# Short convolution and pool taken into the input projection, columns in another order, weight units spread anew

## The chip, the cores and the metric

The kernel runs on one core of one Trainium2 chip. The metric is the device time of one execution in microseconds (us). The engines are PE (TensorE, matrix products), DVE (VectorE), ACT (ScalarE), POOL (GpSimd) and SP (SyncE, here a queue of DMA issues). They run side by side and wait for each other by semaphores.

## The reference

One inference step of a hybrid decoder layer, for a prompt of 512 tokens and eight samples of one token, all in fp32. All 520 tokens go through the same weights. What matters here:

```python
u = RMSNorm(h) @ W_in                 # 2048 -> 3848 columns
z, xbc, dt, u5, gate_b, gate_c, hv, upool = split(u)
y_ssd = SSD(causal conv of xbc, dt) * silu(z)
y_s5  = S5(u5), gelu, gated by sigmoid(y @ w_glu + b)
y_sc  = gate_b * causal_dwconv(gate_c * hv, 3 taps)
y_pool = (mean over windows 2, 4, 8, 16 of upool - upool) @ pool_w * pool_scale
m = concat of the four, each 512 wide, each RMS-normed
h = h + m @ W_out
mem_k, mem_v = RMSNorm(mem) @ W_k, RMSNorm(mem) @ W_v      # 256 tokens, prompt
h = h + CrossAttention(h, mem_k, mem_v or the samples' caches)
h = h + relu(RMSNorm(h) @ W_up)^2 @ W_down
```

Outputs are y of both groups and the new states, among them the last rows of `gate_c * hv` and of `upool`.

## The kernel before

**The weight pipeline.** A product in fp32 is made of three: high part by high part, high by low and low by high. The weights come in units of 512 KB. SP loads a unit into one of two buffers `raw` (`load`, lines 589 to 640), ACT copies its high part to `whi` (`hi_units`, `hi_slots`, `hi_first`, lines 785, 799 and 790), POOL subtracts to get `wlo` (lines 728 and 734; one of the first units is done by DVE), and PE multiplies. `whi` and `wlo` have four slots each. A unit's load waits until both parts of the unit that was in its buffer are made; ACT waits until PE is done with the slot. Each engine works through its own fixed program, so a step that waits holds up all behind it.

**The beginning.** SP loads the first chunk of the tokens, two weight units, then the other three chunks. PE turns the gains, then the tokens, k = 0 to 15 (lines 1445 to 1450); DVE copies each turned piece to `xT` and makes the low part `xl`; ACT makes the high part `xh` (line 824) and the squares for the norm (`x_squares`, lines 834 and 838). Two steps behind, PE multiplies kk = k - 2 by the first two tiles of the weights (line 1476), four units held at once. ACT makes the last two of these at k = 4 and 5.

**The projection.** Behind that, tile t is 128 columns by 520 tokens in two units of 48 matmuls (line 1391). The loop over n = 4 to 51 on PE, DVE and POOL is one unit each; tile 4 + n // 2 ends at odd n. DVE evicts it from PSUM (`evict_u`: times `rB`, the norm) to `stg`, ACT stores it to DRAM (`uscr`). PE may not begin a tile until the tile before the last is evicted. Columns come in the order S5, then short convolution's B, C and HV, pool, Z, XBC. Into the loop are put the four parts of S5: PE makes weights at S5_A = 8, 16, 24, 32 (n), sums at S5_B = A + 2, rows at S5_C = A + 4 (lines 1530 and 1534); DVE makes the complex states (`s5_states`, at S5_B) from which the rows are made, with the table `turn` of powers, built by `doubling` at n = 5 and 19 us long. POOL makes the parts' input weights.

**Keys and values.** Then 64 units of `w_v` and `w_k` (`kv_units`, line 1553), each 12 matmuls of 512 columns, are spread by hand between the steps of the mixers: the gate of S5 (line 1766), turning, `ea` (line 1800), pool products (line 1810), norms and chunk states. DVE does the convolution of XBC from loaded columns, gates, four short convolutions (`short_conv`, rows loaded back from `uscr` to `scb`), four groups of pool rows (`pool_rows`, loaded back to `pu`), and evictions. Both pairs of buffers have two turns, so the loads of groups 2 and 3 wait for groups 0 and 1. ACT's program mixes weight copies with these loads, with squares and roots.

The end of the loop and of that stretch is `w_out`, from about 765 us on; everything behind is unchanged.

Of the kernel before, what the change touches and what calls it, by code (L numbers as in the profile page):

```python
# [16 lines left out]
F32 = mybir.dt.float32  # L17
# [51 lines left out]
S5_B = [n + 2 for n in S5_A]  # L69
S5_C = [n + 4 for n in S5_A]  # L70
MEM_AT = [45, 47, 49, 51]

# [60 lines left out]
def build(nc, io, consts_ap, outs):  # L133
# [31 lines left out]
    with ctx:  # L165
# [42 lines left out]
        dte = at("dte", [NH, 3, TOK], R_H + 16640)  # L208

# [28 lines left out]
        rho = at("rho", [P, 4, NCH], BU + 22592)  # L238
# [8 lines left out]
        scb = at("scb", [P, 2, 4, 524], R_A + 45824)  # L247
# [14 lines left out]
        pu = at("pu", [P, 2, PH + TOK + 1], BU + 8320)  # L262
        pt = at("pt", [P, 2, PH + TOK + 1], BU + 12608)
        pt2 = at("pt2", [P, 2, PH + TOK + 1], BU + 16896)
        plw = at("plw", [P, GT, P], BU + 21184)
# [146 lines left out]
        s.sc_done = sem("sc_done")  # L412
# [5 lines left out]
        s.sc_in0 = sem("sc_in0")  # L418
        s.sc_in1 = sem("sc_in1")
        s.pu0 = sem("pu0")  # L420
        s.pu1 = sem("pu1")
# [108 lines left out]
        sc_in = (s.sc_in0, s.sc_in1)  # L530
        pu_in = (s.pu0, s.pu1)
# [42 lines left out]
        def in_row(t):  # L574

            return C_U5 + P * t if t < 20 else P * (t - 20)
# [6 lines left out]
        def _(sp):  # L583
# [40 lines left out]
            load_first(1)  # L624
            load_tokens(1)
# [11 lines left out]
            with sp.Fori(1, 10) as p:  # L637
                load_pair(p, io["w_in"], 256 * p + C_U5)
            with sp.Fori(0, 3) as p:
                load_pair(p + 10, io["w_in"], 256 * p)  # L640
            sp.wait_ge(s.s5_y, 4)
            for i in range(2):
                sp.dma_start(mnat[:, i, :], io["mem"][P * i:P * i + P, :]).then_inc(s.mem_in, 16)
            with sp.Fori(3, 5) as p:
                load_pair(p + 10, io["w_in"], 256 * p)
# [130 lines left out]
        def _(act):  # L776
# [62 lines left out]

            act.wait_ge(s.row_tr, 1)  # L840
# [116 lines left out]
            def s5_toeplitz(f):  # L957

                act.wait_ge(s.fp_st, 16 * (f + 2))
                for i in range(LC):  # L960
# [36 lines left out]
            def store_tile(t):  # L997

                act.wait_ge(s.tile_free, t + 1)
                src = stg[:, t % 2, :] if t >= 6 else (sqt[:], ssq[:])[t % 2]  # L1000
                dma(uscr[in_row(t):in_row(t) + P, :], src, pj[t % 2])
# [28 lines left out]
            for T in range(3, T_KV + 1):  # L1030
# [6 lines left out]
                if T == 5:  # L1037
                    act.wait_ge(s.dt_ask, 1)
                    act.activation(dte[:, 1, :], dte[:, 1, :], ACT.Exp).then_inc(s.dt_act, 1)
# [7 lines left out]

            def load_short(i):
                for j, c0 in enumerate((C_C, C_HV, C_B)):
                    o = 2 if j == 0 else 0  # L1050
                    dma(scb[:, i % 2, j, o:o + TOK], uscr[c0 + P * i:c0 + P * i + P, :], sc_in[i % 2])

            def load_pool(i):
                dma(pu[:, i % 2, PH:PH + TOK], uscr[C_POOL + P * i:C_POOL + P * i + P, :], pu_in[i % 2])
# [6 lines left out]
            load_short(0)  # L1061
            load_short(1)
# [1668 lines left out]
```

## Time and profile before

| | us |
|---|---|
| median of 3 runs | 2927.6 |
| lowest and highest | 2925.55 and 2928.62 |
| the profiled execution | 2924.35 |
| its span in the trace | 2922.2 |
| PE busy | 2827.7 (97%) |
| DVE, ACT, POOL busy | 886.3, 784.5, 1193.2 |

The profile shows one execution. The span runs from its first instruction to its last; 2.15 us lie around it. "Granted clock" is the TensorE clock that the chip allowed, as a share of full speed. In the chain of work that ended last each step is followed back to what released it. A wait names the engine, the line that waited and what released it. PE at 97% is a mean: it hides that nearly all idle time lies before 675 us.

### The profile page before, as it was taken

Reading aid. Unit: us, or ns where it says so; the run is one execution under the profiler, and the core shown is the slowest. Engines: PE = TensorE matmul, PEld = TensorE weight load, DVE = VectorE, ACT = ScalarE, POOL = GpSimd, SP = SyncE. Lnnn points to the kernel's source line nnn. Section 1 sums busy time; section 2 is a strip of 40 time slices with the busy share of each in tenths; the row PEclk is TensorE's granted clock in tenths of the full one; section 3 lists DMA queues with packets and bytes.
Section 4 is the critical chain, followed back from the end, with each engine's and each line's share of the span. In section 5 each row is a group of like instructions: output and inputs, shape, how many; then the busy total and the mean of one; then the engine's idle time right before and its main releaser. Section 6 shows DMA issues by size and latency. Waiting matters only on the chain.

```text
span 2922.2 us, 54159 instructions
## 1 busy us (share of the span) xinstructions
PE 2827.7 (97%) x22196; PEld 2699.3 (92%) x22196; DVE 886.3 (30%) x1313; ACT 784.5 (27%) x992; POOL 1193.2 (41%) x516
## 2 busy tenths in 40 slices
PE   7999998789899999999999999999999999999998
PEld 5989997576799988779999999999999999999998
DVE  4666517956522334522211000110001100011223
ACT  5221125234332211222232212222112321133222
POOL 1545334546344322334344444444444444443441
PEclk9999999899999999999999999999999999999999
DMA  6744444535433565533233333323333333333332
GB/s 173 138 114 121 115 137 165 169 130 164 160 100 93 150 202 191 193 103 92 81 101 91 90 91 94 93 87 94 93 91 89 93 93 92 88 93 93 87 92 94
DMA packets 510351, 338.36 MB, mean 116 GB/s; under 512 B 31525, under 2 KB 459411, under 8 KB 508815
## 3 DMA queue, kind: packets, MB, share of 16 engines
q1 hardware_dynamic: 470488, 294.02, 34.3%
q10 hardware_dynamic: 39771, 43.04, 5.0%
q8 instruction: 67, 1.10, 0.2%
q14 instruction: 25, 0.20, 0.0%
HBM read 313.28 MB, written 24.02 MB: 115 GB/s over the span
## 4 chain that ended last, share of the span: by engine, by line
PE 81%; issue 9%; POOL 5%; DVE 3%; DMA 1%; ACT 1%; ACTq 0%; POOLq 0%; SPq 0%; DVEq 0%
PE lin L1391 75%; POOL wlo L728 5%; DMA raw<-in_w_in 1%; PE aux L1644 1%; PE aux L1689 1%; PE lin L1584 1%; PE aux L1635 1%; DVE turn L1965 0%; DVE rot L1965 0%; ACTq L802 0%; PE aux L1534 0%; PE aux L1530 0%; PE lin L1476 0%; DVE ca L1965 0%; PE aux L1956 0%
## 5 line engine op out<-in xcount | busy, mean ns | idle before, releaser
L728 POOL TENSOR_TENSOR wlo<-raw,whi 128x1024 fp32r<-128x1024 f32 x472 | 1139.2, 2416 | 1649.8 <-ACT whi L799 1348.7
L799 ACT ACTIVATE whi<-raw 128x1024 fp32r<-128x1024 f32 x384 | 405.9, 1059 | 1438.4 <-PE lin L1391 1298.4
L1391 PE MATMUL lin<-fl,whi 128*128 128x260 f32 x2048 | 578.4, 282 | 0.0
L1391 PE MATMUL lin<-fh,wlo 128*128 128x260 f32 x2048 | 578.0, 282 | 0.0
L1391 PE MATMUL lin<-ml,whi 128*128 128x260 f32 x2048 | 577.6, 282 | 0.0
L1391 PE MATMUL lin<-fh,whi 128*128 128x260 f32 x2048 | 577.6, 282 | 0.0
L1391 PE MATMUL lin<-mh,whi 128*128 128x260 f32 x2048 | 577.5, 282 | 0.0
L1391 PE MATMUL lin<-mh,wlo 128*128 128x260 f32 x2048 | 577.3, 282 | 0.0
L1391 PEld LDWEIGHTS lin<-fh,wlo 128*128 128x128 f32 x2048 | 385.9, 188 | 0.0
L1391 PEld LDWEIGHTS lin<-mh,wlo 128*128 128x128 f32 x2048 | 385.6, 188 | 0.0
L1391 PEld LDWEIGHTS lin<-ml,whi 128*128 128x128 f32 x2048 | 385.5, 188 | 0.0
L1391 PEld LDWEIGHTS lin<-fh,whi 128*128 128x128 f32 x2048 | 385.3, 188 | 0.0
L1391 PEld LDWEIGHTS lin<-mh,whi 128*128 128x128 f32 x2048 | 385.2, 188 | 0.0
L1391 PEld LDWEIGHTS lin<-fl,whi 128*128 128x128 f32 x2048 | 385.2, 188 | 0.0
L1391 PE MATMUL lin<-xh,whi 128*128 128x260 f32 x896 | 256.3, 286 | 5.9 <-DVE stg L1965 5.9
L1391 PE MATMUL lin<-xl,whi 128*128 128x260 f32 x896 | 254.3, 284 | 0.0
L1391 PE MATMUL lin<-xh,wlo 128*128 128x260 f32 x896 | 254.0, 283 | 0.0
L1965 DVE TENSOR_TENSOR h<-lin,h 128x520 f32 (+1 forms) x96 | 67.2, 700 | 582.3 <-PE lin L1391 573.2
L1965 DVE TENSOR_TENSOR fl<-hsq,fh 128x520 f32 x64 | 72.6, 1135 | 476.7 <-ACT fh L1333 476.7
L1391 PEld LDWEIGHTS lin<-xh,whi 128*128 128x128 f32 x896 | 169.9, 190 | 8.3 <-DVE stg L1965 6.4
L1391 PEld LDWEIGHTS lin<-xh,wlo 128*128 128x128 f32 x896 | 170.0, 190 | 0.0
L1391 PEld LDWEIGHTS lin<-xl,whi 128*128 128x128 f32 x896 | 169.9, 190 | 0.0
(417 smaller groups left out, 4380.1 us busy)
## 6 DMA issues: line engine op xcount, KB each, us to landing
raw<-in_w_up SPq DMA_DIRECT2D x128, 512.0 KB, 4.0
raw<-in_w_down SPq DMA_DIRECT2D x128, 512.0 KB, 3.9
raw<-in_w_in SPq DMA_DIRECT2D x60, 512.0 KB, 3.8
raw<-in_w_v SPq DMA_DIRECT2D x32, 512.0 KB, 3.7
raw<-in_w_k SPq DMA_DIRECT2D x32, 512.0 KB, 3.7
raw<-in_w_out SPq DMA_DIRECT2D x32, 512.0 KB, 3.9
raw<-in_w_q SPq DMA_DIRECT2D x32, 512.0 KB, 4.0
piece<-in_cache_mem_k SPq DMA_DIRECT2D x32, 512.0 KB, 6.1
```

What stands on the lines that cost most here:

```text
L728: pool.tensor_tensor(wlo[:, slot, :], raw[:, slot % 2, :], whi[:, slot, :].bitcast(F32), ALU.subtract).then_inc(s.w_lo, 1)
L799: act.activation(whi[:, slot, :], raw[:, slot % 2, :], ACT.Copy).then_inc(s.w_hi, 1)
L1391: mm = pe.matmul(lin[:, 2 * i + f, 0:HALF], w, m[:, k, HALF * f:HALF * f + HALF], start=(n == 0 and part == 0), stop=(n == KT - 1 and part ...
L1584: mm = pe.matmul(lin[:, 2 * i + f, 0:HALF], w, m[:, k, HALF * f:HALF * f + HALF], start=(k == 0 and part == 0), stop=(k == KT - 1 and part ...
L1635: mm = pe.matmul(aux[32 * j:32 * j + 32, 2, :], pTd[:, m, 32 * b:32 * b + 32], piece[:, j, m, :], start=(g == 0 and m == 0), stop=(g == 1 ...
L1644: mm = pe.matmul(aux[:, 2, 0:NMEM], q[:, f0 + d, P * tt:P * tt + P], kTh[:, d, :], start=(d == 0), stop=(d == 3))
L1689: mm = pe.matmul(aux[:, d % 2, :], vNh[:, m, P * d:P * d + P], pT[:, m, :], start=(m == 0), stop=(m == 1))
L1965: step(v.tensor_tensor(out, a, b, op), sm)
```

## The change

- Order of columns: S5, Z, then C, HV and B of each of the four short-convolution groups in turn, pool, XBC. Only Z and XBC tiles are stored to DRAM: 10 in place of 26.
- The short convolution of group i is done by DVE in the projection, after tiles 9, 12, 15, 18 (n = 11, 17, 23, 29), from tiles evicted straight to `scc` and `scp`; B is multiplied in as its tile is evicted. Pool rows follow tiles 20 to 23 (n = 33, 35, 37, 39); PE does the pool products at n = 37, 39, 41, 43 and DVE evicts them one n later. Loads from DRAM for both are gone.
- S5_B and S5_C of the first part come one unit later, the doubling of `turn` is split over n = 4, 6, 7 and 8, and the state transposes come between the first projection units.
- In the stretch of keys and values the pool products are gone, the units are spread anew (three to a chunk in place of two), sigmoids come in pairs, and squares and roots of the norms stand earlier in ACT's program.
- The beginning: SP waits for the first token chunk before it loads the others; the first weight copy precedes the gains copy, parameters and squares come one step later, the third and fourth copy at k = 8 and 9; DVE makes `xl` of k right after `xT` of k; the first products of kk = 0 and 1 leave out the `wlo` part, which is made up at kk = 2 and 3.

```diff
-S5_B = [n + 2 for n in S5_A]
-S5_C = [n + 4 for n in S5_A]
+S5_B = [11] + [n + 2 for n in S5_A[1:]]
+S5_C = [n + 2 for n in S5_B]
+POOL_AT = [37, 39, 41, 43]
...
+        def in_col(t):
+
+            if t < 4:
+                return C_U5 + P * t
+            if t < 8:
+                return C_Z + P * (t - 4)
+            if t < 20:
+                return (C_C, C_HV, C_B)[(t - 8) % 3] + P * ((t - 8) // 3)
+            return C_POOL + P * (t - 20) if t < 24 else C_XBC + P * (t - 24)
+
+        def stored(t):
+            return 4 <= t < 8 or t >= 24
...
             load_first(1)
+            sp.wait_ge(s.x_in0, 80)
             load_tokens(1)
...
-            hi_first(0)
-            hi_first(1)
             for k in range(KT):
                 x_hi(k)
                 if k == 0:
+                    hi_first(1)
+                if k == 1:
                     parameters()
-                if 1 <= k <= 8:
-                    x_squares(2 * k - 2)
-                    x_squares(2 * k - 1)
-                if k in (4, 5):
-                    hi_first(k - 2)
+                if 2 <= k <= 9:
+                    x_squares(2 * k - 4)
+                    x_squares(2 * k - 3)
+                if k in (8, 9):
+                    hi_first(k - 6)
...
-                if k == 11:
+                if k == 13:
                     root(0)
-                if k == 13:
+                if k == 14:
                     hi_slots(1, (0,))
...
-                    if n % 2 == 1 or n == 6:
+                    if (n % 2 == 1 or n == 6) and stored(2 + (n - 1) // 2):
                         store_tile(2 + (n - 1) // 2)
...
-            for i in range(2):
-                act.wait_ge(pj[i], 16 * 13)
+                act.wait_ge(pj[i], 16 * 5)
...
-                if 1 <= i <= 4:
-                    act.wait_ge(s.glu_mm, i)
...
+                for g in ((i - 1, i) if i in (1, 3) else ()):
+                    act.wait_ge(s.glu_mm, g + 1)
...
-            act.wait_ge(s.sc_done, 1)
-            load_short(2)
-            hi_units(14, 16)
-            act.wait_ge(s.sc_done, 2)
-            load_short(3)
-            hi_units(16, 17)
-            hi_units(17, 18)
+            hi_units(14, 18)
...
+            norm_squares(0, s.glu_y, 1)
+            hi_units(21, 22)
             for f in range(2):
...
-            hi_units(21, 23)
+            hi_units(22, 24)
+            root(1)
+            norm_squares(1, s.tile_free, 20)
+            hi_units(24, 27)
             kv_store(1)
             load_rows(0, 5)
-            for i in (2, 3):
-                act.wait_ge(s.mx_pool, i - 1)
-                pool_tail(i - 2)
-                act.wait_ge(s.tails, i)
-                load_pool(i)
-                hi_units(19 + 2 * i, 21 + 2 * i)
-            hi_units(27, 28)
+            root(2)
+            norm_squares(2, s.pl_ev, 4)
+            hi_units(27, 30)
             load_rows(5, 11)
-            hi_units(28, 30)
+            root(3)
+            hi_units(30, 32)
             load_rows(11, 16)
...
                 if kk == 0:
                     pe.wait_ge(s.par_ev, 7)
+                    pe.wait_ge(s.w_hi, 2)
+                if kk == 2:
                     pe.wait_ge(s.w_lo, 2)
                 if kk == 8:
                     pe.wait_ge(s.w_lo, 4)
...
+                        if kk < 2:
+                            first_products(kk, i, (0, 1))
+                        else:
+                            if 2 <= kk < 4:
+                                first_products(kk - 2, i, (2,))
+                            mm = first_products(kk, i, (0, 1, 2))
...
+            def pool_products(i):
+
+                if i == 0:
+                    pe.wait_ge(s.pl_in, 16)
+                pe.wait_ge(s.mx_pool, i + 1)
+                if i >= 1:
+                    pe.wait_ge(s.pl_ev, i)
+                for f in range(2):
+                    mm = pe.matmul(aux[:, f, 0:HALF], plw[:, i, :], halves(pt[:, i % 2, 0:TOK])[:, f, :],
+                                   start=True, stop=True)
+                mm.then_inc(s.pl_mm, 1)
...
-                kv_units(20 + 2 * i, 22 + 2 * i)
-            kv_units(28, 30)
+            kv_units(20, 22)
             pe.wait_ge(s.ea_act, 4)
             token_sums(1, KT + 4)
-            kv_units(30, 31)
+            kv_units(22, 24)
             token_spread(1)
...
-                kv_units(36 + 2 * c, 37 + 2 * c)
+                kv_units(30 + 3 * c, 31 + 3 * c)
...
-                kv_units(37 + 2 * c, 38 + 2 * c)
+                kv_units(31 + 3 * c, 33 + 3 * c)
...
-            kv_units(44, 46)
+            kv_units(42, 46)
...
-            for k in range(KT + 1):
-                if k < KT:
-                    v.wait_ge(s.x_tr, k + 1)
-                    cp(halves(xT[:, k, :]), x_bank(k), s.x_ev)
-                if k >= 1:
-                    v.wait_ge(s.split_hi, k)
...
+            for k in range(KT):
+                v.wait_ge(s.x_tr, k + 1)
+                cp(halves(xT[:, k, :]), x_bank(k), s.x_ev)
+                v.wait_ge(s.split_hi, k + 1)
...
+                elif t < 20:
+                    i, j = (t - 8) // 3, (t - 8) % 3
...
+                    out = (scc[:], scp[:, 2:2 + TOK], y[:, 8 + i, :])[j]
                 else:
...
+                    out = pu[:, PH:PH + TOK]
+                factor = y[:, 8 + i, :] if 8 <= t < 20 and j == 2 else rB[:]
+                tt(halves(out), lin_tile(t % 2), halves(factor), ALU.mult, s.tile_free)
...
             s5_weights(0)
             for n in range(4, 52):
+                if n == 4:
+                    v.wait_ge(s.xs_st, 64)
+                    doubling(turn, 3, range(3))
+                if n in (6, 7, 8):
+                    doubling(turn, 3, (n - 3,))
+                if n == 9:
+                    state_steps()
                 if n in S5_B:
                     s5_states(S5_B.index(n))
                 if n - 1 in S5_C[0:3]:
                     s5_weights(S5_C.index(n - 1) + 1)
                 if n - 3 in S5_C:
                     s5_y(S5_C.index(n - 3))
                 if n - 1 in MEM_AT:
                     mem_rows(MEM_AT.index(n - 1))
+                if n - 1 in POOL_AT:
+                    pool_out(POOL_AT.index(n - 1))
                 if n % 2 == 1:
+                    tile = 4 + n // 2
+                    evict_u(tile)
+                    if 8 <= tile < 20 and (tile - 8) % 3 == 1:
+                        short_conv((tile - 8) // 3)
+                    if 20 <= tile < 24:
+                        pool_rows(tile - 20, POOL_W[tile - 20])
                 if n == 11:
                     soft_ask()
                 if n in (20, 24, 28, 32):
                     softplus(n // 4 - 5)
```

## Rows read from the trace of the kernel before

**Rows 1.** The page, chain that ended last: shares of the span by engine.

```profile
PE 81%; issue 9%; POOL 5%; DVE 3%; DMA 1%; ACT 1%; ACTq 0%; POOLq 0%; SPq 0%; DVEq 0%
```

**Rows 2.** Stretches: busy time (count) of PE, PEld, DVE, ACT, POOL; clock; DMA share; GB/s.

```profile
0.00:73.00 73.00, 52.49 (x366) 40.68 (x366) 30.98 (x43) 36.88 (x82) 13.12 (x11) 1.00 0.61 174
73.00:186.00 113.00, 104.86 (x890) 102.77 (x886) 81.09 (x157) 27.18 (x37) 56.76 (x29) 0.95 0.61 128
186.00:450.00 264.00, 262.82 (x2312) 258.21 (x2312) 110.72 (x149) 61.03 (x81) 109.42 (x51) 1.00 0.42 118
450.00:520.00 70.00, 60.67 (x276) 49.06 (x276) 59.06 (x84) 38.24 (x45) 33.19 (x14) 0.95 0.60 195
520.00:589.00 69.00, 51.55 (x169) 37.21 (x169) 62.97 (x81) 18.74 (x23) 38.47 (x16) 0.81 0.56 167
589.00:675.00 86.00, 79.33 (x341) 61.17 (x339) 55.28 (x75) 27.78 (x36) 42.62 (x19) 0.94 0.41 135
```

**Rows 3.** Waits of PE, 73 to 186: us in total, times, longest.

```profile
PE lin L1391 <- DVE stg L1965: 5.9, 1, 5.9
```

**Rows 4.** Timeline of DVE near 158: start, duration, line, operation, shapes.

```profile
158.33 0.70 DVE L1965 TENSOR_TENSOR stg<-lin,rB 128x520 f32<-128x520 f32 x1
```

**Rows 5.** Timeline of DVE, 235 to 241, as in Rows 4.

```profile
236.19 2.67 DVE L1965 TENSOR_TENSOR hc<-rot,turn 128x256 f32<-128x256 f32 x1
238.89 0.42 DVE L1965 TENSOR_TENSOR rot<-rot,turn 128x256 f32<-128x256 f32 x1
...
240.02 0.40 DVE L1977 COPY hc<-h 128x32 f32<-128x32 f32 x2
```

**Rows 6.** Timeline of POOL in the same stretch.

```profile
236.18 2.39 POOL L728 TENSOR_TENSOR wlo<-raw,whi 128x1024 fp32r<-128x1024 f32 x1 [4.82 <-ACT whi L799]
```

**Rows 7.** Timeline of PE where these states are taken up.

```profile
240.51 0.63 PE L1530 MATMUL aux<-uc,tw 128*128 128x73 f32 x4
```

**Rows 8.** Timeline of DVE at the third S5 part; brackets: idle before it, releaser.

```profile
281.84 0.70 DVE L1965 TENSOR_TENSOR stg<-lin,rB 128x520 f32<-128x520 f32 x1 [1.73 <-PE lin L1391]
```

**Rows 9.** Timeline of DVE, short convolution 1, from its first product to the next.

```profile
510.23 2.65 DVE L1965 TENSOR_TENSOR scb<-scb 128x520 f32<-128x520 f32 x1
...
516.87 0.70 DVE L1965 TENSOR_TENSOR scb<-scb 128x520 f32<-128x520 f32 x1
```

**Rows 10.** Timeline of DVE, first pool group, to the next one's start.

```profile
553.79 0.07 DVE L2364 MEMSET pu<- 128x15 f32 x1
...
555.78 2.29 DVE L1965 TENSOR_TENSOR pt<-plS,pu 128x8 f32<-128x8 f32 x1
...
558.34 0.07 DVE L2364 MEMSET pu<- 128x15 f32 x1
```

**Rows 11.** Waits of PE, 450 to 675.

```profile
PE lin L1553 <- POOL wlo L728: 10.2, 6, 4.3
...
PE aux L1800 <- DVE smk L1965: 3.9, 1, 3.9
```

**Rows 12.** Groups by line, 450 to 675: count, busy us, mean ns, idle before.

```profile
L728 POOL TENSOR_TENSOR wlo<-raw,whi 128x1024 fp32r<-128x1024 f32 x47 | 116.8, 2492 | 110.7 <-ACT whi L785 107.3 <-ACT whi L799 3.2
...
L785 ACT ACTIVATE whi<-raw 128x1024 fp32r<-128x1024 f32 x44 | 46.0, 1055 | 97.8 <-DMA raw<-in_w_v 33.4 <-DMA raw<-in_w_k 31.7 <-PE lin L1553 15.1
...
L1810 PE MATMUL aux<-pt,plw 128*128 128x260 f32 x16 | 6.6, 552 | 11.5 <-DVE pt L1974 5.8 <-DVE y L1969 5.7
```

**Rows 13.** The page, DMA issues: count, KB, median us from issue to landing.

```profile
raw<-in_w_v SPq DMA_DIRECT2D x32, 512.0 KB, 3.7
```

**Rows 14.** Timeline of PE at the third pool product.

```profile
566.83 1.04 PE L1810 MATMUL aux<-pt,plw 128*128 128x260 f32 x4
```

**Rows 15.** Timeline of PE in the beginning: the first products follow these transposes.

```profile
21.51 0.48 PE L1445 MATMUL aux<-idn,xnat 128*128 128x128 f32 x1 [4.91 <-DVE xl L1974]
```

**Rows 16.** Timeline of ACT in the beginning.

```profile
45.15 0.61 ACT L834 ACTIVATE xsq<-xnat 128x512 f32<-128x512 f32 x1
...
47.86 0.73 ACT L824 ACTIVATE xh<-xT,gains 128x520 fp32r<-128x520 f32 x1
```

More of the change, by code:

```diff
@@ L1126, in _, with norm_squares @@
             act.wait_ge(s.ss_st, 16 * 5)
+            def norm_squares(j, ready, count):
+                act.wait_ge(ready, count)
+                for i in range(4):
+                    act.wait_ge(s.ss_done, KT + 4 * j + max(i - 1, 0))
+                    act.activation((sqt, hsq)[i % 2][:], y[:, 4 * NORM_ORDER[j] + i, :], ACT.Square).then_inc(s.sq_done, 1)
+            norm_squares(0, s.glu_y, 1)
+            hi_units(21, 22)
             for f in range(2):
@@ L1459, in _, with first_products @@
                     mm.then_inc(s.stat_mm, 1)
+                def first_products(kk, i, parts):
+                    slot = 2 * i + kk // 8
+                    wh = whi[:, slot, P * (kk % 8):P * (kk % 8) + P]
+                    wl = wlo[:, slot, P * (kk % 8):P * (kk % 8) + P]
+                    for part in parts:
+                        w, m = ((wh, xh), (wh, xl), (wl, xh))[part]
+                        for f in range(2):
+                            mm = pe.matmul(lin[:, 2 * i + f, 0:HALF], w, m[:, kk, HALF * f:HALF * f + HALF],
+                                           start=(kk == 0 and part == 0), stop=(kk == KT - 1 and part == 2))
+                    return mm
                 kk = k - 2
@@ L1470, in _ @@
                     for i in range(2):
-                        slot = 2 * i + kk // 8
-                        wh = whi[:, slot, P * (kk % 8):P * (kk % 8) + P]
-                        wl = wlo[:, slot, P * (kk % 8):P * (kk % 8) + P]
-                        for part, (w, m) in enumerate(((wh, xh), (wh, xl), (wl, xh))):
-                            for f in range(2):
-                                mm = pe.matmul(lin[:, 2 * i + f, 0:HALF], w, m[:, kk, HALF * f:HALF * f + HALF],
-                                               start=(kk == 0 and part == 0), stop=(kk == KT - 1 and part == 2))
+                        if kk < 2:
[4 more added lines that the diff above has]
+                            mm = first_products(kk, i, (0, 1, 2))
                         if kk == 7 and i == 0:
@@ L1710, in _ @@
             mm.then_inc(s.dt_mm, 1)
-            for n in range(1, 4):
-                w_in_unit(n)
+            w_in_unit(1)
             pe.wait_ge(s.st_in, 80)
@@ L1745, in mem_turn @@
                     mm.then_inc(s.mem_tr, 1)
+            def pool_products(i):
[4 more added lines that the diff above has]
+                    pe.wait_ge(s.pl_ev, i)
+                for f in range(2):
+                    mm = pe.matmul(aux[:, f, 0:HALF], plw[:, i, :], halves(pt[:, i % 2, 0:TOK])[:, f, :],
+                                   start=True, stop=True)
+                mm.then_inc(s.pl_mm, 1)
             for n in range(4, 52):
-                for at_, what in ((S5_A, s5_weights), (S5_B, s5_sums), (S5_C, s5_rows), (MEM_AT, mem_turn)):
+                for at_, what in ((S5_A, s5_weights), (S5_B, s5_sums), (S5_C, s5_rows), (POOL_AT, pool_products),
+                                  (MEM_AT, mem_turn)):
                     if n in at_:
@@ L1892, in _ @@
             pe.wait_ge(s.mixn, 16)
[L1893 removed]
+            pe.wait_ge(s.tails, 1)
             for i in range(4):
@@ L2101, in doubling @@
             def doubling(tabl, k0, steps):
-                step(v.memset(tabl[:, 0, :, 0:1], 1.0))
-                step(v.memset(tabl[:, 1, :, 0:1], 0.0))
-                for k in range(steps):
+                if 0 in steps:
+                    step(v.memset(tabl[:, 0, :, 0:1], 1.0))
+                    step(v.memset(tabl[:, 1, :, 0:1], 0.0))
+                for k in steps:
                     n = 1 << k
```

241 lines of the change are left out of this document (95 added, 146 removed).

## Prediction

> **What bounds the kernel now.** I read the chain of work that ended last first: PE carries 81% of it, POOL and DVE 8% together [rows 1]. So time moves only where PE waits, where it runs at the lower clock, or where it gets more work. The table by stretch says where that is [rows 2]. From 186 to 450 us (projection) PE is busy 262.8 of 264 us at clock 1.00: nothing can be won there, and any wait put in counts fully. From 73 to 186 it is idle 8.1 us at clock 0.95; from 450 to 675 (memory keys and values beside the mixers) 9.3, 17.5 and 6.7 us, together 33.5 us, at 0.95, 0.81 and 0.94. These clocks are means of the two levels 1.2 and 2.4 GHz. The change touches 0 to 675 us alone. Third, the waits of PE by releaser in both stretches [rows 3, 11], and the timelines around each moved step [rows 4 to 10, 14 to 16].
>
> **A price for the clock.** A mean of 0.95 over 113 us is 5.7 us of full-speed work lost, for 8.1 us of idle time, 0.7 per idle us; from 450 to 675 the loss is 3.5 + 13.1 + 5.2 = 21.8 us for 33.5, 0.65 per idle us [rows 2]. Part of that low clock lies in the idle time itself, so 0.65 is an upper end and 0 the lower. I take 0.4 for single waits in dense work and 0.65 in the stretch where waits follow each other.
>
> **Beginning (0 to 73 us): 0, from -5 to +8.** Before, the transposes of k=2 wait 4.91 us for DVE's first low parts, and the first products follow right after [rows 15]. With the first token chunk loaded alone, the gains copy behind only one weight copy, and no `wlo` in the first products, they start 4 to 5 us sooner: -5 is the lower end. But `hi_first(3)` now stands on ACT after k=9 and its squares. ACT before spends 2.7 us on one k's two squares and rows (45.15 to 47.86) [rows 16]; then the copy of 1.06 and POOL's subtraction of 2.5 us [rows 12] come before the wait of kk=8 for the fourth `w_lo`, and the third copy, 1.06, one k earlier. That chain is 7.3 us; PE's own work on one k, which before keeps pace with ACT's 2.7, covers as much of it. A wait of about 4.6 us plus hand-overs takes back what the start gave. DVE also waits for ACT between its two steps of each k now; unknown, and covered by +8.
>
> **First S5 part (73 to 186 us): -10.5.** The 5.9 us wait is for the eviction `stg` at 158.33, queued behind the whole doubling of `turn` [rows 3, 4]. With the doubling spread over n = 4, 6, 7, 8 and S5_B at 11, I take 7.5 of the 8.1 idle us as gone, and 0.4 x 7.5 = 3.0 of clock. Ends: 5.9 and 12.5. The state transposes move between two units and wait for nothing that is late.
>
> **DVE steps moved into the full projection: +30.8, from +14 to +42.** The tiles' stores to DRAM and the loads back vanish, off PE's path, worth 0. What counts is DVE's queue.
> Part 1 of S5: DVE ends the states at 240.42 (240.02 + 0.40) and PE takes them at 240.51 [rows 5, 7]: no slack. `short_conv(1)` (n=17) now stands ahead of them. From its first product to the next one's is 6.64 us, of which 1.95 (2.65 against 0.70) is a stretched operation [rows 9]; so +4.7 clean, 6.6 held. I take 6.5, since POOL subtracts all along here.
> Part 2: DVE idles only 1.73 us before the eviction ahead of these states [rows 8], and `short_conv(2)` comes before: 4.7 - 1.7 = 3.0 to 6.6 and, with a further held operation of 2.1 [rows 10], 8.7. I take 6.
> Part 3: `pool_rows(0)` in front: 4.55 us from start to start, 2.3 less 0.18 of it held [rows 10]: 2.4 to 5.3; I take 5.
> `pool_products(1)` and `(2)` wait for `pool_out`, which is queued behind the next `pool_rows` on DVE; two units are some 11 us (2312 matmuls in 264 us, 48 to a unit [rows 2]), against two `pool_rows` with evictions in that time, so 0 to 6; I take 4.5.
> Sum 22.0, and 0.4 x 22 = 8.8 of clock: 30.8. Only S5's rows and the pool products wait on PE for it; evictions are behind them in the same queue. Low end 10.1 (all clean) x 1.4 = 14, high end 26.6 plus 0.6 of clock each, 42.
>
> Why an operation is held: `hc` with two SBUF inputs took 2.67 us beside a POOL subtraction of 2.39 us that began 0.01 us earlier, its twin right after 0.42 [rows 5, 6]. The Trainium skill (SBUF — State Buffer, the section "SBUF: two separate sides") says that DVE operations with two SBUF inputs and GpSimd operations exclude each other for a whole instruction. The trace agrees, 2.67 against 0.42 us. It speaks against this change: by that rule each POOL subtraction met costs about its own 2.4 us, and the first of the waits above would be 4.7 + 2.4 = 7.1 in place of 6.5, the sum 0.8 more.
>
> **Pool products moved into a stretch that PE fills: +4.2**, four at 1.04 us [rows 14]. They go from the later stretch below.
>
> **Memory keys and values (450 to 675 us): -20.4, from -28 to -7.**
> Gone: the products themselves, 6.6 busy, and their waits, 11.5 [rows 12]; the 3.9 us wait for `smk`, since four short convolutions no longer stand before it on DVE, and of the 10.2 us of waits for `wlo` some 6.4 (4.3 is the longest), since weight copies no longer queue behind pool loads and tails on ACT [rows 11]. Together 21.8 us of waits.
> New: on ACT the weight copies 22, 27 and 30 stand behind eight DMA issues, behind `root(2)` with four squares, and behind `root(3)`. No row shows these; the longest wait that a late `wlo` makes now is 4.3 [rows 11], so 0 to 12.9. I take 11.6, near the upper end, as these units come with fewer other PE steps between them.
> The clock: 0.65 x (21.8 - 11.6) = 6.6 back. Weights must arrive faster than now: +3, from 0 to 6. Sum: -6.6 - 21.8 + 11.6 - 6.6 + 3 = -20.4. Up to about 515 us DVE's convolution paces the stretch, and I give it nothing.
> The floor is the chain of one weight buffer: 3.7 landing [rows 13], 1.06 copy, 2.49 subtraction [rows 12], 7.25 us over two buffers, 3.6 a unit. The stretch takes 225 us for 47 units, 4.8 each, and would take 4.35.
>
> **The sum.** 0 - 10.5 + 30.8 + 4.2 - 20.4 = +4.1 us. The profiled execution took 2924.35 us (span 2922.2, 2.15 around it), 3.25 below the median of 2927.6. So 2924.35 + 4.1 + 3.25 = 2931.7 us.
>
> **The rivals.**
> B: POOL doesn't hold the moved steps, and they cost their bare time. For it: the steps are cheap, and POOL works only 109 of 264 us there [rows 2]. Against: both the convolution and the pool rows measured had a held operation [rows 9, 10]. It gives 14.1 in place of 30.8, and if ACT's order costs 8.6 in place of 11.6, 2931.7 - 16.7 - 3 = 2912.
> C, on the slower side: the stretch of keys and values does not give the time back. With DVE's waits gone, the weight chain and ACT's order set the pace: waits on `pt`, `y` and `smk` turn into waits on `wlo`. It decides once PE asks for a unit faster than about 4.5 us. Gone are then 6.6 + 11.5 + 3.9, new are 11.6 + 3, and no clock comes back: -7.4 in place of -20.4, which is 2944.7. For it: `wlo` is the largest single releaser there already [rows 11]; against: ACT is busy 85 of 225 us, POOL 114 [rows 2].
> D: the beginning doesn't do what the change says: the wait for the fourth `w_lo` costs 8 us more than the start gives, 2939.7. For it: nothing but squares fills ACT there [rows 16].
>
> **How the numbers follow.** A measurement of this kernel can tell 0.2%, 5.9 us, from no change: the band is 2921.7 to 2933.5. My forecast has 0.50, with a range of its own of 2920 to 2944 (its terms' bounds, not all at once): 0.05 faster, 0.24 same, 0.21 slower. B has 0.27 (0.24 faster, 0.03 same), C 0.15 (all slower), D 0.08 (0.01, 0.02, 0.05). That makes 0.30 faster, 0.29 same, 0.41 slower. The range goes from 2902, B with the first S5 part at its end of 12.5 and the beginning at -5, to 2950, C with a beginning that loses 5.
>
> **What would show it.** The beginning: the first product before 20 us, and a wait of about 5 us on `wlo` near 45 us. First S5 part: no wait on `stg` from 73 to 186, the stretch 10 us shorter. Projection: PE waits on `hc` or `s5o` at n = 20, 28, 36 of 5 to 6 us each, and on `y` before the second and third pool product; without these waits B holds. Keys and values: no waits on `pt` and `smk`; if those on `wlo` grow beyond 20 us, C holds. The prediction is wrong if PE waits in the projection stay under 12 us, or if the later stretch shortens by less than 10 or over 30 us.

## The result and the profile after

The change makes the kernel slower: 2958.4 us median of 4 runs (2955.5 to 2961.2) against 2928.1 (2925.6 to 2929.2), a ratio of 1.011 with a 95% interval of 1.0097 to 1.0122. The profiled execution took 2961.2 us, its span is 2959.1; the one before had 2922.2. So the two traces differ by 36.9 us, the medians by 30.3.

The chain that ended last, by engine, in the profile after (before: [rows 1]):

```profile
PE 80%; issue 8%; DVE 5%; POOL 5%; DMA 1%; ACT 1%; SPq 0%; POOLq 0%; DVEq 0%; ACTq 0%
```

DVE's share of the chain has risen from 3% to 5%. The stretches after, columns as in [rows 2]:

```profile
0.00:73.00 73.00, 52.22 (x313) 43.04 (x316) 27.28 (x42) 35.99 (x81) 10.15 (x9) 0.95 0.61 173
73.00:186.00 113.00, 113.00 (x994) 109.76 (x986) 86.39 (x149) 30.62 (x40) 62.36 (x31) 0.97 0.61 130
186.00:450.00 264.00, 233.42 (x1854) 225.62 (x1854) 153.52 (x214) 39.71 (x50) 93.83 (x43) 0.88 0.33 87
450.00:520.00 70.00, 67.07 (x487) 63.74 (x486) 19.91 (x36) 25.46 (x37) 26.25 (x11) 0.95 0.38 122
520.00:589.00 69.00, 63.94 (x287) 49.32 (x286) 52.17 (x71) 35.69 (x45) 35.69 (x16) 0.98 0.42 129
589.00:675.00 86.00, 68.99 (x308) 54.21 (x306) 34.85 (x55) 27.02 (x34) 43.76 (x19) 0.94 0.49 152
```

From 186 to 450 us PE is now busy 233.4 of 264 us, 262.8 before, at a clock of 0.88 in place of 1.00 [rows 2]. That is where the time went. PE waits there for `hc`, the complex states, and for `y`, into which DVE evicts the pool products; before, its waits on `hc` were 0.9 us or less, and there was none on `y`. Now, from 186 to 460 us:

```profile
PE aux L1518 <- DVE hc L1967: 23.6, 4, 6.9
PE aux L1744 <- DVE y L1959: 7.0, 2, 4.9
```

Four waits on `hc`, one for each part of S5, and two on `y`, before the second and third pool product. They are 30.6 us together. From 460 to 765 us:

```profile
PE lin L1541 <- POOL wlo L735: 26.6, 17, 3.8
```

The waits on `pt`, on `y` and on `smk` of [rows 11, 12] are gone, and waits on `wlo` have grown to 26.6 us; before they were 13.4 in the same window. From the first unit of keys and values to the last the stretch went from 308.3 to 293.6 us, but PE still waits 39.1 us in it, 41.2 before: waits on `wlo` took the place of those on DVE. What it gave back is the pool products, 6.6 us, and some 6 us of clock, 0.95 in place of 0.91.

**Where the 36.9 us lie.** The two kernels do the same steps in nearly the same order, so a step's start in both traces tells how far one is behind. I took three: the products for `dt` after the beginning (101.99 before, 105.01 after), the sums of S5's part 0 (172.56 and 172.99; after, one unit more of 5.9 us lies before them), and the first transposes of the memory tokens, which stand at unit 45 in both. The latter in the timeline of PE, before and after:

```profile
405.83 0.93 PE L1744 MATMUL aux<-idn,mnat 128*128 128x128 f32 x7
```

```profile
457.06 0.71 PE L1733 MATMUL aux<-idn,mnat 128*128 128x128 f32 x5
```

| stretch | after less before | predicted |
|---|---|---|
| beginning, to the `dt` products | +3.0 | 0 (-5 to +8) |
| to the sums of part 0 | -8.5 | -10.5 |
| from there to unit 45: moved steps and pool products | +56.7 | +35.0 |
| behind unit 45: keys and values | -14.3 | -20.4 |
| sum | +36.9 | +4.1 |

Three terms are about what was forecast, and one is 22 us off. What stands in it: waits of 30.6 us, less 1.2 that were there before; four pool products, 3.1 (what they add below in the kernel with the same work one unit later, where PE doesn't wait around them); and the rest, 24.2 us, for which PE ran, but at the lower clock.

**How a moved step becomes a wait.** The timeline of DVE around part 1, from the first product of `short_conv(1)` to its last, the start of the states, a held operation among them, and the last copy:

```profile
232.61 0.70 DVE L1955 TENSOR_TENSOR scp<-scp,scc 128x520 f32<-128x520 f32 x1
...
238.52 0.70 DVE L1955 TENSOR_TENSOR y<-y,rB 128x520 f32<-128x520 f32 x1
239.26 0.29 DVE L1967 COPY rho<-s5p 128x256 f32<-128x256 f32 x1
...
246.09 2.54 DVE L1955 TENSOR_TENSOR hc<-rot,turn 128x256 f32<-128x256 f32 x1
...
251.18 0.40 DVE L1967 COPY hc<-h 128x32 f32<-128x32 f32 x2
```

The convolution takes 6.6 us (232.61 to 239.26), the states start behind it and end at 251.58. PE needed them at 244.8. The timeline of PE there, brackets as in [rows 8]:

```profile
251.63 1.13 PE L1518 MATMUL aux<-uc,tw 128*128 128x73 f32 x4 [6.84 <-DVE hc L1967]
252.69 1.13 PE L1522 MATMUL aux<-hc,ca 64*128 64x73 f32 x8
```

It waits 6.84 us, and then each group of the rows takes 1.13 us. Before, the first took 0.63 [rows 7]. The clock in the 8.6 us of these rows and in the 11.8 behind them, columns as in [rows 2]:

```profile
251.60:260.20 8.60, 8.57 (x49) 7.52 (x49) 4.51 (x3) 0.00 (x0) 0.00 (x0) 0.50 0.00 0
260.20:272.00 11.80, 11.80 (x84) 11.80 (x85) 4.55 (x6) 1.78 (x3) 2.39 (x1) 0.83 0.22 47
```

0.50 is the lower of the two levels, 1.2 GHz, and 0.83 a mix of both. The rows take 8.6 us in place of the 4.8 they took before (+3.8), and 0.17 of the next 11.8 us is 2.0 more: 5.8 us for the clock, behind a wait of 6.8.

In part 2 the convolution is not directly ahead of the states, but the queue is: three rows of DVE, the convolution's first product, its last, and the eviction of the next tile:

```profile
285.96 0.70 DVE L1955 TENSOR_TENSOR scp<-scp,scc 128x520 f32<-128x520 f32 x1
...
296.89 0.70 DVE L1955 TENSOR_TENSOR y<-y,rB 128x520 f32<-128x520 f32 x1
...
306.03 0.70 DVE L1955 TENSOR_TENSOR y<-lin,y 128x520 f32<-128x520 f32 x1
```

11.7 us for the convolution (4.7 clean), then 8.4 for the softplus's second part; the states start only at 306.8, 7.2 us after PE's sums were done at 299.6.

Part 0's wait of 5.1 us has no short convolution and no pool rows ahead of it. Ahead are the last two doublings, beside POOL's input weights, and the state steps; three rows of them:

```profile
163.28 1.17 DVE L1955 TENSOR_TENSOR etmp<-turn,ang 128x256 f32<-128x256 f32 x1
...
170.29 2.77 DVE L1955 TENSOR_TENSOR turn<-turn,etmp 128x512 f32<-128x512 f32 x1
...
174.67 2.47 DVE L1955 TENSOR_TENSOR etmp<-h,s5p 128x128 f32<-128x128 f32 x1
```

Operations of 128 x 256 that took 0.43 us before take 1.17 while POOL works through six operations of 1.1 to 1.4 us each; the two others shown are held for 2 us.

### The profile page after: what moved, and what is told of

Its sections match the earlier page's. It is cut to its first block, busy times and chain, and to the rows that moved or that the text cites. A ratio compares the mean times of both kernels' runs of the same rounds, so it can differ in the third digit from the quotient of the medians.

```text
span 2959.1 us, 53927 instructions
## 1 busy us (share of the span) xinstructions
PE 2843.5 (96%) x22196; PEld 2716.6 (92%) x22196; DVE 884.6 (30%) x1311; ACT 776.2 (26%) x984; POOL 1192.5 (40%) x516
## 4 chain that ended last, share of the span: by engine, by line
PE 80%; issue 8%; DVE 5%; POOL 5%; DMA 1%; ACT 1%; SPq 0%; POOLq 0%; DVEq 0%; ACTq 0%
PE lin L1366 73%; POOL wlo L735 5%; PE aux L1632 1%; PE aux L1677 1%; DVE turn L1955 1%; PE lin L1445 1%; PE lin L1572 1%; DVE rot L1955 1%; PE aux L1518 1%; PE aux L1522 1%; PE aux L1623 1%; DVE pt L1955 0%; DVE hc L1955 0%; DMA raw<-in_w_in 0%; DVE etmp L1955 0%
```

## The experiments

All times are medians. Each comparison gives the ratio to the kernel before, run on the same chip. That kernel took 2926.3 to 2928.7 us in the three sets of runs below and 2928.1 above, so a difference in us between kernels of different sets is good to some 2 us, as here between the changed kernel and the others. Two theories were to be told apart first. Theory 1: the steps moved into the projection stand ahead of S5's states in DVE's queue, PE waits, and the clock falls after each wait. Theory 2: the rest of the change, order of columns, positions and products, makes the loss.

**The moved arithmetic left out.** This kernel does not compute the short convolutions and the pool rows, nor the product with B at the eviction; of each step one short operation and the copy of the new state remain.

```diff
             def short_conv(i):
...
-                tt(p[:, 2:2 + TOK], p[:, 2:2 + TOK], scc[:], ALU.mult)
+                cp(o[:, 0:8], p[:, 2:10])
                 cp(scn[:, i, :], p[:, SEQ:SEQ + 10])
-                ts(o[:, 0:SEQ], p[:, 2:2 + SEQ], scw[:, i, 2:3])
...
             def pool_rows(i, w):
...
-                stt(o[:, 0:SEQ], src[:, PH:n], 1.0 / w, u[:, PH:n], ALU.mult, ALU.subtract)
...
+                ts(o[:, 0:TOK], u[:, PH:PH + TOK], 1.0 / w, sm=s.mx_pool)
```

> The changed kernel with the arithmetic of the short convolutions and of the pool rows left out on DVE (one short copy, or one scaling of the tile, stays of each, so all waits and hand-overs are kept; the outputs that hang on them are not computed). Theory 1, DVE's queue: the waits of PE on hc of parts 1 to 3 (6.8, 6.9, 4.8 us) and on y (7.0) go, the one of part 0 (5.1) stays, since no moved step stands ahead of it; with 0.7 us of clock for each that is 25.5 x 1.7 = 43 us, near 2915. Theory 2, the other parts of the change (order of columns, part 0 one unit later, stores and products in other places) make the loss: at most 10 us faster than the changed kernel, 2948 or more.

Measured: 2920.2 us, ratio 0.998 (0.997 to 0.999), 38 us faster than the changed kernel. The waits on `hc` were 4.8 us in part 0 and 1.2, none worth naming and 1.2 in the others, those on `y` were gone. Theory 1 holds: with the other parts of the change all in place, the loss is gone. Theory 2 falls.

**The same work, one unit later.** Nothing is left out here.

```diff
                 if n in S5_B:
                     s5_states(S5_B.index(n))
+                if n in (12, 18, 24, 30):
+                    short_conv(n // 6 - 2)
...
                 if n - 1 in POOL_AT:
                     pool_out(POOL_AT.index(n - 1))
+                if n in (34, 36, 38, 40):
+                    pool_rows(n // 2 - 17, POOL_W[n // 2 - 17])
                 if n % 2 == 1:
                     tile = 4 + n // 2
                     evict_u(tile)
-                    if 8 <= tile < 20 and (tile - 8) % 3 == 1:
-                        short_conv((tile - 8) // 3)
-                    if 20 <= tile < 24:
-                        pool_rows(tile - 20, POOL_W[tile - 20])
```

> The changed kernel with each short convolution and each group of pool rows one unit later in DVE's program, so that they stand behind the complex states of parts 1 and 3; nothing is left out. Theory 1, the place in the queue: the waits on hc of parts 1 and 3 go (6.8 and 4.8 us), part 0 and part 2 keep theirs; 11.6 x 1.7 = 20 us faster, near 2938. Theory 2, the amount of DVE work and POOL's holding set the wait wherever the steps stand: under 8 us faster, 2950 or more.

Measured: 2926.5 us, ratio 1.0008 (0.9998 to 1.0017): 32 us faster than the changed kernel, with the same work. The waits of PE from 186 to 460 us:

```profile
PE aux L1518 <- DVE hc L1967: 12.6, 2, 6.9
```

Parts 0 and 2 are left, 5.8 and 6.9. It gained more than the 20 expected, because both waits on `y` went too (7.0): `pool_out` now stands ahead of the next `pool_rows`. The sum is 18.6 us of waits, and some 13 us of clock, which is the rest and agrees with the traces (13.6 us in the stretches behind these waits). The loss is one of order in a queue.

**The softplus behind the states of part 2.**

```diff
-                if n in (20, 24, 28, 32):
-                    softplus(n // 4 - 5)
+                if n in (20, 27, 29, 43):
+                    softplus((20, 27, 29, 43).index(n))
```

> As the kernel before it in this set, and the second part of the softplus moves from unit 24 to 27, the third to 29 and the fourth to 43, behind the states of part 2 (and 3). Theory 1: the wait on hc of part 2 (6.9 us) goes too, another 11 us, near 2927. Theory 2, part 2 waits for the short convolution ahead of it and not for the softplus: no more than 3 us beyond the kernel before it.

Measured: 2920.1 us, ratio 0.9976 (0.9967 to 0.9986), 6.4 faster than the kernel before it in this set, and faster than the kernel before the change. The waits:

```profile
PE aux L1518 <- DVE hc L1967: 4.6, 1, 4.6
PE aux L1733 <- DVE y L1959: 2.4, 1, 2.4
```

The gain lies between the two theories' 11 and 3 us, but the wait of part 2 is gone, as theory 1 said, and its rows end 10.9 us sooner. A new wait of 2.4 us, before the memory transposes, gave some of it back, the stretch of keys and values the rest.

**What a wait costs, in the kernel before.** Seven scratch operations of 0.76 us ahead of the states of parts 1 to 3:

```diff
+                for _ in range(7 if f else 0):
+                    tt(ctmp[:], ctmp[:], ctmp[:], ALU.max)
                 cp(rho[:], s5p[:, 6, w].unsqueeze(2).to_broadcast([P, 4, NCH]))
```

> The kernel before, and seven more operations of 0.76 us on a scratch tile ahead of the complex states in parts 1, 2 and 3: 5.3 us of DVE work each, more where POOL holds one. It measures what a wait of PE in the full projection costs. PE's waits should be about 5.2, 3.6 and 5 us, 14 in all. Theory 1, a wait costs about 0.7 us of clock for each us: +24. Theory 2, the price of the prediction, 0.4: +19. Theory 3, the wait alone: +14.

Measured: 2970.1 us, ratio 1.015 (1.0133 to 1.0167), +43.7 us (38.3 of it in the stretch of the table below); far above each theory. The waits were 6.8, 8.3 and 6.9 us, not 14 together but 22.0. The same loop with 1, 2 and 4 operations:

> The kernel before with 1, 2 and 4 operations of 0.76 us ahead of the complex states in parts 1, 2 and 3: waits of PE of about 0.7, 1.6 and 3 us. It tells what the clock costs at each length. A price by the us (0.7): 5.3 x 1.7 = +9. A price by the event: nothing after the 0.7 us wait, about 5 us after each of the others, whatever its length, +14 to +16.

Measured: 2953.0 us, ratio 1.0081 (1.0064 to 1.0098), +24.5. The waits were 1.2, 4.6 and 5.5 us. The rows that follow the first two in the timeline of PE:

```profile
243.09 0.67 PE L1530 MATMUL aux<-uc,tw 128*128 128x73 f32 x4 [1.17 <-DVE hc L1977]
243.69 0.67 PE L1534 MATMUL aux<-hc,ca 64*128 64x73 f32 x8
```

```profile
301.82 1.13 PE L1530 MATMUL aux<-uc,tw 128*128 128x73 f32 x4 [4.60 <-DVE hc L1977]
302.88 1.13 PE L1534 MATMUL aux<-hc,ca 64*128 64x73 f32 x8
```

The clock while these rows ran, in the same columns as in [rows 2]:

```profile
243.10:247.90 4.80, 4.80 (x49) 4.20 (x49) 4.73 (x3) 0.00 (x0) 2.35 (x1) 1.00 0.38 116
301.80:310.40 8.60, 8.58 (x49) 7.53 (x49) 4.02 (x7) 0.00 (x0) 0.00 (x0) 0.50 0.31 94
```

After 1.17 us of waiting the rows run at full speed, after 4.60 at half. With 2, 1 and 2 operations:

> The kernel before with 2, 1 and 2 operations of 0.76 us ahead of the states in parts 1, 2 and 3, for waits of about 2, 1.5 and 2.5 us. A price of the clock by the event that sets in above some 1.2 us: each costs 4 to 6 us more than itself, +18 to +24 in all. A price that grows with the wait: +9 to +11.

Measured: 2955.5 us, ratio 1.0092 (1.0072 to 1.0113), +26.8; the waits were 4.1, 3.9 and 4.1 us. The stretch from the end of part 0's rows to the memory transposes took 214.4 us before and in these three kernels:

| kernel | longer by | waits more by | rest, the clock | waits of 3.9 us and more | each |
|---|---|---|---|---|---|
| seven operations | 38.3 | 21.7 | 16.6 | 3 | 5.5 |
| 1, 2 and 4 | 22.2 | 10.9 | 11.3 | 2 | 5.6 |
| 2, 1 and 2 | 27.7 | 11.7 | 16.0 | 3 | 5.3 |

So ahead of S5's rows the clock's price goes by the wait, and not by its length. Taken one by one, from the rows' first matmul to PE's next need of DVE, less what this took before, the eight waits of 3.9 to 8.3 us cost 4.2 to 6.1 us each on top of themselves; the longest cost 5.7, the shortest 6.1. In the changed kernel the four waits on `hc` cost about as much, but the fifth long one, 4.9 us on `y`, only 2.4. Behind it come a pool product and projection matmuls, and no S5 rows. The same holds for the 5.9 us wait on `stg` in the kernel before, which projection matmuls follow. The clock behind each, the kernel before first, then the changed one:

```profile
159.10:163.20 4.10, 4.10 (x19) 4.10 (x20) 3.96 (x5) 3.14 (x5) 2.58 (x2) 0.50 0.35 132
163.20:186.00 22.80, 22.45 (x207) 22.01 (x206) 16.19 (x22) 3.44 (x4) 16.59 (x10) 1.00 0.54 138
```

```profile
429.90:434.90 5.00, 4.96 (x19) 4.60 (x20) 0.00 (x0) 0.00 (x0) 0.00 (x0) 0.50 0.37 104
434.90:445.00 10.10, 10.10 (x85) 10.07 (x85) 1.46 (x2) 1.08 (x2) 2.39 (x1) 1.00 0.17 49
```

PE works 4 to 5 us at half speed there, and loses 2.0 and 2.4 us. Behind the eight waits ahead of S5's rows it works 10.2 to 14.0 us at half speed. The place differs between the two kinds and no run changes it alone, so it isn't shown that the rows are the reason; the traces show only that the two kinds differ.

For short waits the length doesn't decide at all: waits of 1.2 and 1.4 us were followed by no fall in the kernel with 1, 2 and 4 operations and in the last one below. In the one with the arithmetic left out the rows behind two waits of 1.2 us took 7.6 and 6.0 in place of 4.8 us, and from these rows on to PE's next need of DVE it took 4.4 and 3.1 us more.

Why do operations of 0.76 us make a wait of 3.9? The timeline of DVE in part 2 of the last kernel:

```profile
292.05 1.42 DVE L1965 TENSOR_TENSOR ctmp<-ctmp 128x576 f32<-128x576 f32 x1
293.50 2.38 DVE L1977 COPY rho<-s5p 128x256 f32<-128x256 f32 x1
...
299.12 3.52 DVE L2205 TENSOR_TENSOR_SCAN rot<-rho,rot 128x256 f32<-128x256 f32 x2
...
305.64 2.42 DVE L1977 COPY hc<-h 128x32 f32<-128x32 f32 x2
```

Unheld, these take 0.76, 0.29, 1.42 and 0.40 us. One operation more shifts all that follow against POOL's subtractions: they are held by 0.7, 2.1, 2.1 and 2.0 us, 6.9 together, where in the kernel before three operations of this part were held by 1.0, 1.0 and 2.1. That is 2.8 us more, and with the 0.76 it is the 3.6 us by which the wait grew from 0.3 to 3.9.

**POOL's other work moved away.** The changed kernel, with POOL's input weights three units later:

```diff
-                if n - 3 in S5_A[0:3]:
-                    input_weights(S5_A.index(n - 3) + 1)
+                if n - 6 in S5_A[0:3]:
+                    input_weights(S5_A.index(n - 6) + 1)
```

> The changed kernel (2958.4 us) with POOL's input weights of parts 1 to 3, six operations each, three units later in POOL's program, away from the short convolutions and the softplus. Theory 1, POOL holds the moved steps: short convolution 2 takes under 8 us in place of 11.7, and the wait on hc of part 2 falls from 6.8 to some 3 us; 3 to 5 us faster. Theory 2, only the place in the queue counts, and another POOL operation takes over the holding: under 2 us.

Measured: 2965.9 us, ratio 1.0124 (1.0103 to 1.0144), 7.5 us slower than the changed kernel. The first row of short convolution 2, the first one behind it (the softplus), and three of the states, in the timeline of DVE:

```profile
287.82 0.70 DVE L1955 TENSOR_TENSOR scp<-scp,scc 128x520 f32<-128x520 f32 x1
...
294.46 0.69 DVE L1955 TENSOR_TENSOR hsq<-hsq,sqt 8x520 f32<-8x520 f32 x1
...
311.35 1.17 DVE L1955 TENSOR_TENSOR rot<-rot,turn 128x256 f32<-128x256 f32 x1
312.55 1.17 DVE L1955 TENSOR_TENSOR hc<-hc,rot 128x256 f32<-128x256 f32 x1
...
318.71 2.41 DVE L1967 COPY hc<-h 128x32 f32<-128x32 f32 x2
```

The convolution took 6.6 us in place of 11.7, as theory 1 said of it, but neither theory had the kernel slower. The input weights now lie beside the states, whose operations took 1.17 in place of 0.42: the wait of part 2 rose from 6.8 to 8.1 us, that of part 1 from 6.8 to 10.4. The holding is real, and it goes wherever POOL's work goes. The Trainium skill (SBUF — State Buffer, "SBUF: two separate sides") says that the one of the two that starts first keeps the shared ports for its whole instruction. The trace agrees here: 1.17 us is about one POOL operation of 1.12 us. It gives no rule for how many meet; only the timeline does.

**The beginning.** On the kernel of 2920.1 us:

```diff
-                if k in (8, 9):
-                    hi_first(k - 6)
+                if k in (6, 7):
+                    hi_first(k - 4)
```

> The kernel with the moved steps behind the states and the softplus later (2920.1 us), and the third and fourth weight copies on ACT at k = 6 and 7 in place of 8 and 9, when their loads have just landed (35.8 and 37.4 us). Theory 1: the 6.4 us wait of PE on the fourth wlo at 51 us goes; ACT gives some of it back, as its copies now delay the squares: 3 to 7 us faster, near 2915. Theory 2: ACT paces the beginning by its squares and high parts, and PE's wait only moves to the low parts: within 2 us.

Measured: 2912.3 us, ratio 0.995 (0.9934 to 0.9967), 7.8 faster, a little over theory 1's 3 to 7. In the changed kernel PE waited here at 51 us:

```profile
51.66 0.58 PE L1445 MATMUL lin<-xh,whi 128*128 128x260 f32 x1 [6.39 <-POOL wlo L741]
```

The largest wait of PE up to 120 us, but for that on the first tokens, is now

```profile
PE aux L1418 <- DVE xl L1964: 3.2, 3, 1.5
```

Theory 1 holds. ACT's order cost the beginning what the earlier start had won.

**Part 0 later still.** On the kernel of 2920.1 us, S5_B of part 0 at 12:

```diff
-S5_B = [11] + [n + 2 for n in S5_A[1:]]
+S5_B = [12] + [n + 2 for n in S5_A[1:]]
```

> The same kernel (2920.1 us) with the sums and rows of S5's part 0 one unit later once more (units 12 and 14). Theory 1: the wait of 4.6 us on hc goes, since DVE needs 5.5 us for one more unit's time, and with it the clock's fall: with a price by the event (some 5 us after any wait of more than about 1.2 us, as the rows after such waits took 8.5 in place of 4.8 us) 9 to 10 us faster, near 2911; with a price of 0.4 by the us, 6.5 faster. Theory 2: DVE's queue is full up to there and the wait stays: within 2 us.

Measured: 2919.5 us, ratio 0.9967 (0.9953 to 0.9981): no difference, and the wait stayed at 4.6 us. It was not the doubling alone. The three operations of `soft_ask` (unit 11) came ahead of the states, and a scan and a product among these were held. With `soft_ask` moved to unit 13 too, and all mends together:

```diff
-S5_B = [11] + [n + 2 for n in S5_A[1:]]
+S5_B = [12] + [n + 2 for n in S5_A[1:]]
...
-                if k in (8, 9):
-                    hi_first(k - 6)
+                if k in (6, 7):
+                    hi_first(k - 4)
...
-                if n == 11:
+                if n == 13:
                     soft_ask()
```

> All mends together: moved steps behind the states, softplus later, weight copies at k = 6 and 7 (2912.3 us so far), S5's part 0 at units 12 and 14, and the three operations that ask for the softplus at unit 13 in place of 11, since with part 0 later they stood ahead of its states (177.1 to 179.9 us) and kept the wait at 4.6 us. Theory 1: the wait falls under 1.5 us, and the clock's fall goes with it, 5 us; 8 to 10 us faster, near 2903. Theory 2, the states themselves take longer than two units with what POOL holds: the wait stays above 3 us, 2910 or more.

Measured: 2906.6 us, ratio 0.9919 (0.9900 to 0.9937), 0.8% faster than the kernel before. The waits of PE on DVE that are left up to 460 us in S5's rows and before the memory transposes:

```profile
PE aux L1733 <- DVE y L1959: 2.3, 1, 2.3
...
PE aux L1518 <- DVE hc L1967: 1.4, 1, 1.4
```

None in part 0. The gain over the kernel of 2912.3 us was 5.7 us by the medians; the intervals of the two ratios, some 5 us to each side, can't tell this from the 8 to 10 expected. Part 1 now waits 1.4 us, with no fall of the clock. With units 12 and 14 alone the wait had stayed; moving `soft_ask` alone was not run, so which share is whose stays open.

**Keys and values.** On the kernel of 2920.1 us, the low parts of half of each unit's columns are not made, for the memory keys and values only:

```diff
+                    pool.tensor_tensor(wlo[:, slot, 0:512], raw[:, slot % 2, 0:512], whi[:, slot, 0:512].bitcast(F32),
+                                       ALU.subtract).then_inc(s.w_lo, 1)
```

> The same kernel (2920.1 us), and for the units of memory keys and values POOL subtracts only the first half of each unit (the low parts of the other half are not computed), 1.2 us in place of 2.4. Theory 1, the weight chain paces that stretch (landing 3.7, copy 1.06, subtraction 2.4, 7.2 us for two buffers, 3.6 a unit against 2.8 of PE): the 27 us of PE's waits on wlo fall by more than half, 12 to 20 us faster. Theory 2, ACT's order (roots, squares, issues) makes these waits: they stay above 20 us and the time changes by less than 6 us.

Measured: 2892.1 us, ratio 0.9879 (0.9862 to 0.9895), 28 us faster, more than theory 1's 12 to 20. The waits from 460 to 765 us, 27.3 us before this edit:

```profile
PE lin L1549 <- POOL wlo L776: 8.1, 6, 2.9
```

The same edit in the kernel before:

> The kernel before (2928.1 us) with POOL's subtraction halved for the units of memory keys and values, as in the changed order, where it gave 28 us. Theory 1: before the change DVE's steps pace that stretch, and the weight chain became the bound only when they left it: under 12 us faster. Theory 2: the chain bounds both kernels alike: 20 us or more.

Measured: 2904.5 us, ratio 0.9918 (0.9898 to 0.9938), 24 us faster; waits of 9.0 in place of 13.4:

```profile
PE lin L1561 <- POOL wlo L769: 9.0, 4, 5.2
```

The time is theory 2's, but its reason isn't shown here. The waits on `wlo` fell by 4.4 us only. A shorter subtraction also holds DVE less, and DVE's same 300 instructions between the first and the last unit (kernel before, then this one) show it, 221.8 us busy against 176.4:

```profile
452.60:760.60 308.00, 266.83 (x1134) 204.18 (x1134) 221.76 (x300) 127.30 (x150) 159.75 (x64) 0.91 0.49 156
453.40:740.60 287.20, 256.97 (x1134) 199.03 (x1134) 176.44 (x300) 126.54 (x150) 91.20 (x64) 0.93 0.54 166
```

In the changed order the weight chain is what PE waits for: there 19.2 of the 20.9 us by which PE's waits fell were on `wlo`, though DVE was freed as well (159.3 to 130.5 us busy). Before the change both are at work, and this run doesn't part them.

## Why the prediction was wrong

It forecast 2931.7 us, 2902 to 2950; the time is 2958.4.

- **Beginning: right within its range.** Forecast 0, with a wait of about 5 us on the fourth `wlo`; it was 6.4, the first product came at 19.9 us, and the stretch cost 3.0. Two weight copies two steps sooner take 7.8 us off.
- **First S5 part: right in sign and about in size, -8.5 against -10.5; the waits were not foreseen.** The wait on `stg` went. But the sum took the idle time as gone and did not ask what DVE must do before part 0's states. The doubling had only been moved; with POOL's input weights beside it it ended later, and the rows waited 5.1 us.
- **Moved steps: the step that failed, +56.7 against 35.0, with an upper end of 46.2.** Their place, ahead of the states of parts 1, 2 and 3 and of `pool_out`, was right, and so was each wait's size nearly: 6.8, 6.9, 4.8 and 7.0 us, against 6.5, 6, 5 and 4.5. With part 0's they are 30.6 against 22.0. What was mis-sized is the clock: 0.4 us per us of wait, at most 0.65. It was 24.2 us in place of 8.8, for the four waits on `hc` about 5 us each, whatever their length. Part 0's wait, 5.1 us and 5.5 of clock, stood in the sum at nothing.
- **Why the clock's price came out low.** The loss of 5.7 us in [rows 2] is clock over the whole stretch from 73 to 186 us, and part of it falls into the idle time, as the prediction said. Behind the 5.9 us wait [rows 3] PE worked 4.1 us at half speed: 2.0 us lost, 0.35 per us, so 0.4 was right for that wait. The step that failed is carrying it over to waits that stand ahead of S5's rows, where PE stayed at half speed for 10 us and more. The `y` waits, 2.7 us of clock for 7.0, were not far off it. No row of the kernel before showed a long wait ahead of S5's rows; the longest there was 0.9 us.
- **Keys and values: right within its range, -14.3 against -20.4.** The products and the clock came back as forecast (6.6 and some 6 us), the waits did not: -2 us in place of -7.2. The weight chain sets the pace, which is rival C's mechanism, though C had no clock come back and -7.4 in all. Its sign, waits on `wlo` above 20 us, is met from 460 to 765 us (26.6) and missed from 450 to 675 (18.0).
- **Rivals.** B (bare durations, no holding) is excluded: the convolutions took 6.6 and 11.7 us for 4.7. C alone did not decide, D did not happen. No case held what came: every forecast wait real, and those ahead of S5's rows each followed by a long fall of the clock. Between the two traces the miss is 36.9 - 4.1 = 32.8 us: clock of the moved steps with part 0's 15.4, waits 7.4 more (part 0's 5.1 among them), keys and values 6.1, the beginning 3.0, the first S5 part 2.0, less 1.1 for the pool products. The medians show 6 us less of it, as the profiled execution before lay 3.3 us below the median that the forecast used, and the one after 2.7 above its own.

## What to carry to other kernels

When work moves to an engine that "has time", ask at each place who waits for what stands next in its queue: the same steps one unit later were worth 32 us, at no cost in work. Price a wait of a dense TensorE stretch as an event, its own length and a fall of the clock behind it, and read that price from a wait that the same work follows, not from a stretch's mean and not from a wait at another place: here it was about 5 us ahead of S5's rows and about 2 ahead of projection matmuls. An engine that shares a resource stretches moved work in proportion to how it meets the other one, so leave slack of two or three such meetings, not the bare duration.

## What the runs showed that I had not expected

- The price of a wait does not grow with its length: ahead of S5's rows 4.2 to 6.1 us for waits from 3.9 to 8.3 us. The rows behind one run at a granted clock of 0.50 for 8.6 us. Two waits of 4.9 and 5.9 us that pool or projection matmuls follow cost about 2 us.
- One operation of 0.76 us on DVE, with no slack behind it, made PE wait 3.6 us more, 3.9 for 0.3, because it changed which of DVE's operations meet POOL's.
- Halving POOL's subtraction in 64 units gave 24 us in the kernel before and 28 in the changed order, though POOL is busy only about half of that stretch. In the changed order what counts is its place in the chain of load, copy and subtraction over two buffers; before the change the time for which it holds DVE may count as much.
